# A hybrid encoder step: sample tokens moved to the second token group, their token-form products split over four column groups

## What is computed

```
h   = rmsnorm(x) * (1 + scale1) + shift1          # per stream
q, k, v, gate, decay = h @ w_in (columns)          # mixer A: gated linear attention, 4 heads, state 128 x 256
dq, dk, dv           = h @ w_in (columns)          # mixer B: two softmax maps a head, 8 heads, rotary
x   = x + gate1 * (merge of A and B) @ w_out
h2  = rmsnorm(x) * (1 + scale2) + shift2
idx = 16 best of 128 x 128 product keys, 8 heads   # 128 experts a token
y   = x + gate2 * sum_k softmax_k * gelu(h2 . u[idx_k]) * v[idx_k]
```

## Time and profile before

| | us |
|---|---|
| median of 3 runs | 4312.25 |
| lowest, highest | 4308.04, 4312.65 |
| span of the profiled execution | 4303.9 |
| PE busy in it | 3099.8 |
| DVE busy | 2705.5 |
| ACT busy | 1511.1 |
| POOL busy | 1254.2 |
| DMA | 1499.17 MB, 348 GB/s over the span |

### The profile page before, as it was taken

The page is one execution under the profiler, slowest core; times in us unless marked ns, Lnnn a source line. Parts: engine busy times, 40 slices in busy tenths (PEclk is TensorE's granted clock), DMA queues, the critical chain, the costliest instruction groups (busy, mean ns, idle before and its releaser), DMA issues. The chain is left out here.

```text
span 4303.9 us, 48708 instructions
## 1 busy us (share of the span) xinstructions
PE 3099.8 (72%) x15864; PEld 1982.7 (46%) x15864; DVE 2705.5 (63%) x7617; ACT 1511.1 (35%) x3085; POOL 1254.2 (29%) x1068
## 2 busy tenths in 40 slices
PE   6787798887788769778887679768776677733333
PEld 4676565665555337455554347444433254400000
DVE  1326357337667884477668873577678945776775
ACT  3533366312255651114555540223446611010010
POOL 0000111112233332333223332333334323355553
PEclk8888888898888779898888889888778788855555
DMA  7485767687989989998999899989999999999998
GB/s 261 157 305 189 278 243 267 254 319 307 357 343 375 360 309 390 404 415 354 363 362 366 351 359 384 417 344 402 375 372 386 363 410 415 398 408 415 416 406 336
DMA packets 269363, 1499.17 MB, mean 348 GB/s; under 512 B 44968, under 2 KB 81672, under 8 KB 97464
## 3 DMA queue, kind: packets, MB, share of 16 engines
q0 software_dynamic: 152064, 1107.36, 64.5%
q1 hardware_dynamic: 117048, 388.70, 24.0%
HBM read 1463.49 MB, written 31.36 MB: 347 GB/s over the span
## 5 line engine op out<-in xcount | busy, mean ns | idle before, releaser
L1698 POOL DMA_INDIRECT rt_ring<-in_peer_uv,rt_few_idx x1056 | 1250.9, 1185 | 3021.0 <-PE rt_acc L876 2385.5
L1644 DVE SCALAR_TENSOR_TENSOR rt_ring<-rt_ring,rt_h 128x1024 f32<-128x1024 f32 x1056 | 1265.9, 1220 | 504.7 <-DMA rt_ring<-in_peer_uv,rt_few_idx 481.7
L876 PE MATMUL rt_acc<-rt_ring,rt_diag 128*32 128x512 f32 x4224 | 759.9, 795 | 623.1 <-DVE rt_diag L1655 622.1
L625 PE MATMUL pair<-dense,w 128*128 128x256 f32 (+2 forms) x3056 | 598.6, 355 | 14.0 <-DMA w<-in_weights 12.2
L625 PEld LDWEIGHTS pair<-dense,w 128*128 128x128 f32 x3056 | 518.1, 199 | 128.8 <-issue 64.5
L614 PE MATMUL pair<-w,dense 128*128 128x256 f32 (+1 forms) x2352 | 556.4, 395 | 9.5 <-DVE dense L1300 3.5
L1199 ACT ACTIVATE rt_act_dot<-rt_dot 128x2 f32<-128x2 f32 x528 | 106.1, 202 | 1269.0 <-DVE rt_ring L1644 1262.1
L876 PEld LDWEIGHTS rt_acc<-rt_ring,rt_diag 128*32 128x32 f32 x4224 | 100.1, 122 | 953.4 <-DVE rt_diag L1655 810.1
L614 PEld LDWEIGHTS pair<-w,dense 128*128 128x128 f32 (+1 forms) x2352 | 436.2, 189 | 158.8 <-issue 72.9
L1655 DVE TENSOR_SCALAR rt_diag<-cst,rt_act_dot,rt_few_prob 128x32 f32<-128x32 f32 x1056 | 266.1, 296 | 119.9 <-ACT rt_act_dot L1199 109.5
L625 PE MATMUL bank<-dense,w 128*128 128x256 f32 (+2 forms) x1424 | 276.9, 351 | 1.7 <-DMA w<-in_weights 1.2
(11 more groups left out here) (241 smaller groups left out, 3248.5 us busy)
## 6 DMA issues: line engine op xcount, KB each, us to landing
w<-in_weights SPq DMA_DIRECT2D x284, 1024.0 KB
rt_ring<-in_peer_uv,rt_few_idx POOLq DMA_INDIRECT x1056
dense<-scratch_mod SPq DMA_DIRECT2D x18, 512.0 KB, 12.4
dense<-in_x_prompt SPq DMA_DIRECT2D x16, 512.0 KB, 13.5
rt_h<-scratch_h SPq DMA_DIRECT2D x33, 128.0 KB
rt_x<-scratch_x SPq DMA_DIRECT2D x132, 32.0 KB
out_k_prompt<-dense SPq DMA_DIRECT2D x32, 128.0 KB
out_v_prompt<-dense SPq DMA_DIRECT2D x32, 128.0 KB
```

The source lines that it names most:

```text
L625: mm = nc.tensor.matmul(bank[b][:, 0:n], wt[:, k * CH + j * P:k * CH + (j + 1) * P], src[:, k, 0:n], start=(k == 0), stop=(k == KC - 1))
L876: mm = nc.tensor.matmul(acc[u % 2][a * T:(a + 1) * T, :], diag[b % 2][:, i, :], slot[:, D + c * BANK:D + (c + 1) * BANK], start=(q == 0), ...
L1644: dt = nc.vector.scalar_tensor_tensor(up, up, 1.0, h2[u % 2][:], ALU.mult, ALU.mult, accum_out=dot[:, b % 2, i:i + 1])
L1698: nc.gpsimd.indirect_dma_start(ring[n % RING][:], None, d["peer_uv"], bass.IndirectOffsetOnAxis(ap=few_idx[u % 2][:, c:c + 1], axis=0)).th ...
```

## The change

`SAMPLE = 2`: the sample becomes tile 2, in group 1 with tile 1, and the prompt's tiles 2 to 7 become tiles 3 to 8 (`place(t)` gives their place in the prompt). The sample's retrieval unit becomes unit 8, after tile 1's four. All tests of `t < NT` or `t == NT` are rewritten by `SAMPLE`; keys of group 1 are stored in two pieces; group 1 instead of group 4 has 16 loads of keys and values, of two transfers each for the sample. The prompt's state goes to a new DRAM scratch before the sample's pass and comes back after it; group 2 waits for it. Groups 1 and 2 end 16 steps ahead of their units, groups 3 and 4 24. The sample's own selection ends 24 steps earlier than the rule for a second tile. The sample's 24 token-form products are computed as four partial sums of two matmuls each, one for each column group; ACT copies the 128x256 result to SBUF, and one matmul with stacked identities adds the four, one tick later, after the next tick's product.

```diff
-GROUPS = ((0,), (1, 2), (3, 4), (5, 6), (7, 8))
+SAMPLE = 2
+GROUPS = ((0,), (1, SAMPLE), (3, 4), (5, 6), (7, 8))
...
+def width(t):
+    return DEC if t == SAMPLE else P
+def place(t):
+    return NT if t == SAMPLE else t - (t > SAMPLE)
+def row0(t):
+    return place(t) * P
+UNITS = [(row0(t) + j * T, t, j) for t in range(NT + 1) for j in range(width(t) // T)]
...
-    ends = [0] + [first[g] - (LEAD if g > 1 else LEAD_1) for g in range(1, NG)]
+    ends = [0] + [first[g] - (LEAD if g > 2 else LEAD_1) for g in range(1, NG)]
...
-            n = NB * (COPIES if t < NT else 1)
-            sides.append((tiles[ti + 1], start + 2, start + n - 8, select(tiles[ti + 1], 0)))
+            n = NB * (width(t) // T)
+            early = 3 * NB // 2 if tiles[ti + 1] == SAMPLE else 0
+            sides.append((tiles[ti + 1], start + 2, start + n - 8 - early, select(tiles[ti + 1], 0)))
...
             def tokens(key, wt, ti, src, among):
                 c0, n = ti * P, width(GROUPS[key[1]][ti])
+                if n == DEC:
+                    b, before = take(("quarters",) + key, among)
+                    pe.wait_ge(bank_free[b], before)
+                    for k in range(KC):
+                        q = k % 4
+                        mm = nc.tensor.matmul(bank[b][q * T:(q + 1) * T, 0:CH], src[:, k, c0:c0 + n], wt[:, k * CH:(k + 1) * CH],
+                                              start=(k < 4), stop=(k >= 4))
+                    mm.then_inc(bank_made[b], 1)
+                    return bank_made[b], before + 1
...
+            def join(g, ti, key):
+                if GROUPS[g][ti] != SAMPLE:
+                    return
+                b, before = sessions[("quarters",) + key]
+                pe.wait_ge(bank_free[b], before + 1)
+                b, before = take(key, ALL)
+                pe.wait_ge(bank_free[b], before)
+                nc.tensor.matmul(bank[b][0:DEC, 0:CH], stack, quarters, start=True, stop=True).then_inc(bank_made[b], 1)
...
+                if 0 < n <= 4 * nt:
+                    i, ti = (n - 1) // nt, (n - 1) % nt
+                    join(g, ti, (kind, g, i, ti))
...
+            def quarter(g, ti, key):
+                if GROUPS[g][ti] != SAMPLE:
+                    return
+                if parted[0] is not None:
+                    b, before = sessions[parted[0]]
+                    act.wait_ge(bank_made[b], before + 1)
+                b, before = sessions[("quarters",) + key]
+                act.wait_ge(bank_made[b], before + 1)
+                nc.scalar.activation(quarters, bank[b][:, 0:CH], ACT.Copy).then_inc(bank_free[b], 1)
+                parted[0] = key
...
-                sp.dma_start(d["gla_prompt"][0, 0, heads].rearrange("h k v -> k h v"), state[:, heads, :]).then_inc(st_out, 16)
+                if g == NG - 1:
+                    sp.dma_start(d["gla_prompt"][0, 0, heads].rearrange("h k v -> k h v"), state[:, heads, :]).then_inc(st_out, 16)
+                    return
+                sp.dma_start(d["state"][heads].rearrange("h k v -> k h v"), state[:, heads, :]).then_inc(st_out, 16)
                 sp.wait_ge(st_out, 16 * (2 * p + 1))
                 sp.dma_start(state[:, heads, :], d["state_gla"][0, 0, heads].rearrange("h k v -> k h v")).then_inc(st_in, 16)
...
                 sp.dma_start(d["gla_sample"][0, 0, heads].rearrange("h k v -> k h v"), state[:, heads, :]).then_inc(st_out, 16)
                 sp.wait_ge(st_out, 16 * (2 * p + 2))
+                sp.dma_start(state[:, heads, :], d["state"][heads].rearrange("h k v -> k h v")).then_inc(st_in, 16)
```

More of the change, by code:

```diff
@@ L76, in key_tiles @@
 def key_tiles(t):
-    if t < NT:
-        return [(i, P) for i in range(t + 1)]
+    if t != SAMPLE:
+        return [(i, P) for i in range(place(t) + 1)]
     return [(i, P) for i in range(PAST // P)] + [(PAST // P, DEC)]
@@ L84, in key_count, with key_runs, keys_stored @@
     return sum(n for _, n in key_tiles(t))
+def key_runs(g):
+    if SAMPLE in GROUPS[g]:
+        return [(ti * P, row0(t), width(t)) for ti, t in enumerate(GROUPS[g])]
+    return [(0, row0(FIRST[g]), columns(g))]
+def keys_stored(k):
+    return sum(len(key_runs(i // 4)) for i in range(k % 2, k + 1, 2))
 def kv_loads(g):
-    kinds = [t for t in GROUPS[g] if t == NT or t == max(i for i in GROUPS[g] if i < NT)]
+    kinds = [t for t in GROUPS[g] if t == SAMPLE or t == max(i for i in GROUPS[g] if i != SAMPLE)]
     return [(h, t) for h in range(DH) for t in kinds]
@@ L101, in kv_load_of @@
     per = len(kv_loads(g)) // DH
-    return x // nt * per + (1 if GROUPS[g][x % nt] == NT else 0)
+    return x // nt * per + (1 if GROUPS[g][x % nt] == SAMPLE else 0)
 def weight_order(g):
@@ L139, in transfers @@
         return 1
-    return sum(2 if t == NT else 1 for part, h, t in kv_parts(name[0], name[2]))
+    return sum(2 if t == SAMPLE else 1 for part, h, t in kv_parts(name[0], name[2]))
 def load_count(j):
@@ L324, in sequence @@
     assert nxt == NU and pos == len(lane)
+    done = [i for i in fill] + [i for _, ticked, _ in steps for i, _ in ticked]
+    when = {(i[1], i[2]): n for n, i in enumerate(done) if i[0] == "select"}
+    for n, i in enumerate(done):
+        if i[0] == "keys":
+            assert all(t < 2 or when[t - 2, SELECT - 1] < n for t in GROUPS[i[1]]), i
+    assert all(when[t, 0] > when[t - 1, SELECT - 1] for t in range(1, NT + 1))
     return fill, steps
@@ L507, in gla_units @@
         def gla_units(g, last):
-            return [(ti, t, ti * P, width(t), j) for ti, t in enumerate(GROUPS[g]) if (t == NT) == bool(last) for j in range(2)]
+            return [(ti, t, ti * P, width(t), j) for ti, t in enumerate(GROUPS[g]) if (t == SAMPLE) == bool(last) for j in range(2)]
         def gla_base(g, p, last):
@@ L657, in dv @@
                     released[g, "dv", i] = tokens(("dv", g, i, ti), weights((g, "dv", i)), ti, hT, ALL)
+                if 0 < n <= 4 * nt:
+                    i, ti = (n - 1) // nt, (n - 1) % nt
+                    join(g, ti, ("dv", g, i, ti))
             def gla_qk(kind, g, p, j):
@@ L831, in mix @@
                     released[g, "wo", c] = tokens(("mo", g, c, ti), weights((g, "wo", c)), ti, mT, ALL)
+                if 0 < i <= 4 * nt:
+                    c, ti = (i - 1) // nt, (i - 1) % nt
+                    join(g, ti, ("mo", g, c, ti))
             def shift(g, k):
@@ L1053, in gla_v @@
                     if u == 0 and p == 0:
-                        for i in range(2):
-                            act.wait_ge(kt_out[i], 16 * 2 * (g + 1))
+                        for m in range(2):
+                            act.wait_ge(kt_out[m], 16 * keys_stored(4 * g + 2 + m))
                     act.wait_ge(bank_made[b], before + 1)
@@ L1117, in gla_gate, with mix @@
                                          bank[b].rearrange("p (c t) -> p c t", c=4)[:, :, 0:n], ACT.Copy).then_inc(bank_free[b], 1)
+                if i < 2 * nt:
+                    quarter(g, i % nt, ("gr", g, p, i // nt, i % nt))
+            def mix(g, i):
+                nt = len(GROUPS[g])
+                if i < 4 * nt:
+                    quarter(g, i % nt, ("mo", g, i // nt, i % nt))
             def attend(g, k):
@@ L1217, in select @@
                     nc.scalar.activation(e[:], below[:], ACT.Exp).then_inc(exped, 1)
-            stages = {"norm": norm, "dv": dv, "la": la, "gv": gla_v, "gla": gla, "gr": gla_gate, "at": attend, "merge": merge,
+            stages = {"norm": norm, "dv": dv, "la": la, "gv": gla_v, "gla": gla, "gr": gla_gate, "at": attend, "merge": merge, "mix": mix,
                       "shift": shift, "keys": keys, "dots": dots, "copies": copies, "select": select}
@@ L1624, in select @@
                     for u in range(2):
-                        dve.wait_ge(idx_in[u], 16 * COPIES * 2 * (t - 1))
-                        dve.wait_ge(prob_in[u], 16 * COPIES * 2 * (t - 1))
+                        loaded = sum(v % 2 == u for v in range(NU) if UNITS[v][1] <= t - 2)
+                        dve.wait_ge(idx_in[u], 16 * COPIES * loaded)
+                        dve.wait_ge(prob_in[u], 16 * COPIES * loaded)
                 nc.vector.tensor_copy(idx[t % 2][:], idxf[:]).then_inc(idx_ready, 1)
@@ L1789, in rotary @@
                 if 0 <= u < 4 * nt and u % nt == nt - 1:
-                    i, n = u // nt, columns(g)
+                    i = u // nt
                     k = g * 4 + i
```

95 lines of the change are left out of this document (56 added, 39 removed).

## The result

The change makes the kernel slower by 1.7%: 4380.65 us median (four runs, 4363.63 to 4390.3) against 4312.45, ratio 1.0166, 95% interval 1.0141 to 1.0191. Run again unedited beside other kernels it gave 1.0175 (1.0151 to 1.0200). The profiled execution took 4375.4 us with a span of 4373.3, 69.4 us more than the span before. The forecast was 4343 us, +31.

The account below looks back on a forecast made before the run. The limit was taken to change: PE in window 1, DMA and PE in windows 2 to 4, plain gather steps in window 5. 449+543+730+886+934+793 = 4335, with 8.35 added 4343 us; range 4270 to 4405.

Parts of the forecast that it names:

- Its sign: Whole kernel: slower, 4343 us, +31 on the span; chance 0.42 for this forecast, slower in all 0.60.
- its mechanism: 48 steps moved to the tail cost 247 us; windows 1 and 2 give back some 200, windows 3 and 4 14.
- six terms: Span by stretches of gather steps: fill 449, window 1 543, window 2 730, window 3 886, window 4 934, window 5 793 us.
- the tail: Window 5, gather steps with no dense work beside them: three more units of 82.4 us, 793 us, +247.
- window 1's saving by the quarters: Window 1, 20 quartered sample products: 1.9 us with join instead of 3.63, 35 us saved.
- the copy and the join: Window 1: ACT copy of 0.38 us per quartered product, then the adding matmul; waits costed at 0 to 5 us, taken as 0.
- From `mix` on: Last stretch of window 1 (mix, shift, keys): 127.5 us to become 107.
- The chains: Window 1, sample's longer work between engines: attention eight more ticks, +27 us; recurrence in two passes, +8 each.
- The step price: One more gather step beside dense work costs 2.5 to 2.6 us, against 5.15 in the tail; used to build window 2.
- The faster rival: Window 1 keeps its 74 us idle and loses only PE work: 494 us, total 4294; chance 0.28.
- The rival of dead quarters: Each quartered product stays at its old price plus the join: +44 us, 4387; chance 0.04.
- The slower rival: Sample's chains longer, attention +58 and split +16 in both passes: window 1 at 590, total 4390; chance 0.14.

Follow-up runs that it names:

- experiment 3: Kernel before with the quarters alone: 1.0032; changed kernel with quarters undone: 1.0205; changed kernel with only dk and dq products left plain: 1.0170.
- My own experiment on it: Kernel before with LEAD = 40 instead of 24, moving 16 steps from window 2 into the tail: ratio 1.0021, 4311.84 us.

## Why the prediction came out as it did

Its sign, its mechanism and five of its six terms held: windows 2 to 5 and the fill each came within 5 us of their forecast in the profiled run (the repeat within 10), and the tail, +249 us, is what the change pays. The forecast slowdown, 31 us, was less than half of the measured 68.

**The term that was mis-sized is window 1's saving by the quarters**, "20 of the 24 products fall into window 1, 35 us". PE did save 33. In time they are worth 13 to 17 us, as the run without them shows. That is a shortfall of 18 to 22, against the 24 us by which window 1 missed 543. The prediction had costed the copy and the join "at 0 to 5 us, and take 0", with the prompt's product as cover; for dk and dq there is no gain at all, and in window 4 the same edit cost 7 us. The step that failed is that PE's work was taken to hold nearly every stretch but attention. From `mix` on the prediction took 20 us off (-7, -16, +3), and 4 to 6 came. What follows `mix` ran 10 to 11 us shorter, but `mix` itself 5 to 6 longer. Its four quartered products gave nothing (experiment 3), and DVE waited 17.4 us there for the gate loads, a wait that the prediction had not costed.

**The chains** were sized about right: 27 for attention and 16 for the split recurrence, 43; taken out together they are 44 to 48 us. Without them a window of 500 was forecast, 519 was measured, and that difference is again of the size that the quarters fell short by. The other terms partly cancel: attention grew by 32 to 36 us in the table, not 27, and merge shrank by 40, not 33. Two step counts of the prediction are one off: 2976.2 to 3059.6 us holds 12 steps, not 13, which makes the split 11 instead of 8, and 1435.5 to 1617.1 holds 26, not 25.

**The step price** of 2.55 us beside dense work gave window 2 correctly (730 for 734), since between 80 and 120 steps it is 2.5. As a general price it is wrong: 1.3 to 1.7 in window 1, 3.3 to 4.3 above 104 steps with the deeper attention, 5.2 in the tail. My own experiment on it, with 42 us expected and 9 measured, failed on that.

**The faster rival** needed window 1 at 512 or less. Even with both chains gone it is at 519. **The rival of dead quarters** is out by the rows: 1.45 us a product. With it, the rule of the Trainium skill (TensorE: Matmul & The Clock Gate, "The mechanism"), by which weight loads would not overlap on shared rows, does not show here: 16 loads and 16 matmuls took 1.45 us, 0.2 more than the retrieval's eight matmuls with as many columns in all, and PE has no idle time before them. **The slower rival** had nearly the right size in all (4390) and the wrong reason: window 1 was to be at 590.

A lower clock went with PE's idle time: 0.89 to 0.78 in window 1. No run separates what it cost.

## To carry over

Where one stretch of a kernel runs at a price per step that depends on what lies beside it, a regrouping is worth the difference of two prices; measure them by shifting steps alone, before writing the regrouping. Here 48 steps with nothing beside them cost 249 us, and what they gave back was 155 and 39 in windows 2 and 3, where they had stood, and 16 to 20 in window 1, where the narrow group was to pay for the rest. Work taken from a busy engine counted in full where that engine hardly waited (merge, 41 us of 41), in half over a window where it did, and not at all where another engine waited for a load (`mix`). A narrower group has no fewer handovers between engines.

## What was unexpected

- Column groups made a product of 32 rows 2.5 times cheaper (3.63 to 1.45 us), and the kernel that had only this edit became 0.3% slower (1.0032, 1.0015 to 1.0050).
- 40 gather steps beside a PE-bound group cost 1.3 us each in window 1, a quarter of their 5.2 us in the tail.
- Twelve steps taken out of the tail by a shorter lead gave back 3.7 us each instead of 5.2, because the selection was squeezed into the twelve that were left ahead of a unit.
